# A two-model kernel on one core: other orders for the mixer's tiles, convolution taps, selection rounds and roots

## The reference

```python
def token_mixers(u, ...):                      # first block
    qa, ka, va, qi, ki, wi, qb, kb, vb, gate_a, gate_b = split(u @ w_in)
    # A: per query the 128 keys with the largest index scores (qi, ki, wi), then softmax attention, 8 heads
    # B: (softmax(q1 k1) - lam * softmax(q2 k2)) @ vb, 4 heads
    o_b = rms_norm(o_b, g_subln) * (1 - lam_init)        # over 128 features of a head
    return (sigmoid(gate_a) * (o_a @ w_branch_a) + sigmoid(gate_b) * (o_b @ w_branch_b)) @ w_out

def mixer(x):                                  # second block
    ua, ub, uc, ud = split(rms_norm(x) @ w_in)
    y_a = silu(layer_norm(depthwise_conv31(a * sigmoid(gate))))        # 31 taps, 256 channels
    y_b = rms_norm(bidirectional gated scan of (q, forget zf/zb, v), onorm) * silu(g)
    y_c = gb * depthwise_conv3(gc * xin)                               # 3 taps
    y_d = latent attention(cq, ckv, kr), 4 heads, q and k normed and rotated
    x = x + rms_norm per branch(y_a, y_b, y_c, y_d) @ w_out
    # then cross attention to mem with normed q and k, then the FFN
```

## Time and profile before

| what | us |
|---|---|
| median of 3 runs | 3483.81 (3483.07 to 3484.43) |
| the profiled execution, its own time | 3483.18 |
| its span in the trace | 3481.4 |
| each first-block layer: project, B, latent attention, tail | 165.5, 99.7, 90.7, 539.8 |
| each second-block layer: mixer, attention, tail | 249.7, 49.1, 534.1 (second layer 526.6) |

### The profile page before, as it was taken

One profiled execution on the slowest core, in us unless ns is written; L12 is line 12 of the kernel. 1 busy time (PEld: TensorE's weight loads), 2 busy tenths in 40 slices (PEclk: granted clock), 3 DMA queues, 4 the chain that ended last, 5 costly groups with the idle time before them and its releaser, 6 DMA issues. The chain is left out here.

```text
span 3481.4 us, 39157 instructions
## 1 busy us (share of the span) xinstructions
PE 3182.5 (91%) x14620; PEld 2474.4 (71%) x14620; DVE 1670.7 (48%) x2524; ACT 1435.2 (41%) x2281; POOL 1576.3 (45%) x870
## 2 busy tenths in 40 slices
PE   7978899999998799999999967899999985979999
PEld 6655688878766567887878735578887852758877
DVE  2773347731357533775235883433313785443320
ACT  4736533333384554333343454432223355352221
POOL 4623545544563354554456332334445432234443
PEclk8989999999899999999999978999999997989999
DMA  3111233323211112332322101223333200213333
GB/s 112 61 55 43 69 95 97 97 91 103 76 61 61 37 55 91 103 97 94 103 86 89 52 12 37 66 81 97 96 103 98 67 25 27 65 49 97 97 97 103
DMA packets 73740, 265.09 MB, mean 76 GB/s; under 512 B 8656, under 2 KB 9168, under 8 KB 73168
## 3 DMA queue, kind: packets, MB, share of 16 engines
q1 hardware_dynamic: 73552, 262.59, 24.1%
HBM read 260.46 MB, written 2.10 MB: 75 GB/s over the span
## 5 line engine op out<-in xcount | busy, mean ns | idle before, releaser
L359 POOL TENSOR_TENSOR low<-raw,high 128x1024 fp32r<-128x1024 f32 x482 | 1170.7, 2430 | 1298.8 <-ACT high L350 1276.0
L374 PE MATMUL bank<-slot_r,low 128*128 128x512 f32 (+2 forms) x3636 | 1434.6, 395 | 0.0
L375 PE MATMUL bank<-slot_r,high 128*128 128x512 f32 (+2 forms) x3636 | 1432.1, 394 | 0.0
L373 PE MATMUL bank<-slot_r,high 128*128 128x512 f32 (+1 forms) x3316 | 1339.9, 404 | 100.0 <-POOL low L359 22.5
L350 ACT ACTIVATE high<-raw 128x1024 fp32r<-128x1024 f32 x482 | 507.3, 1054 | 848.2 <-PE bank L375 819.1
L373 PEld LDWEIGHTS bank<-slot_r,high 128*128 128x128 f32 x3316 | 636.5, 192 | 286.5 <-issue 69.4
L374 PEld LDWEIGHTS bank<-slot_r,low 128*128 128x128 f32 (+1 forms) x3636 | 696.4, 192 | 148.9 <-issue 9.2
L375 PEld LDWEIGHTS bank<-slot_r,high 128*128 128x128 f32 (+1 forms) x3636 | 695.4, 191 | 149.8
L1568 DVE SCALAR_TENSOR_TENSOR tmp<-padded,small,tmp 128x512 f32<-128x512 f32 x176 | 209.9, 1251 | 0.0
L834 POOL TENSOR_SCALAR tmp<-tmp,stat 128x512 f32<-128x512 f32 (+3 forms) x128 | 72.0, 562 | 195.4 <-DVE stat L809 167.1
L698 PE MATMUL bank<-slots 64*128 64x256 f32 (+4 forms) x384 | 96.1, 509 | 44.5 <-PEq L320 40.7
(11 more groups left out here) (310 smaller groups left out, 3661.6 us busy)
## 6 DMA issues: line engine op xcount, KB each, us to landing
raw<-w SPq DMA_DIRECT2D x482, 512.0 KB, 3.5
slots<-x_in SPq DMA_DIRECT2D x4, 512.0 KB, 6.6
slots<-mem_in SPq DMA_DIRECT2D x2, 1024.0 KB, 4.9
out<-slots SPq DMA_DIRECT2D x8, 256.0 KB, 4.8
const<-const_in SPq DMA_DIRECT2D x1, 1073.5 KB, 10.6
padded<-p_in SPq DMA_DIRECT2D x2, 512.0 KB, 5.5
tmp<-masks_in SPq DMA_DIRECT2D x1, 512.0 KB, 11.4
small<-small SPq DMA_DIRECT2D x2, 231.5 KB, 2.7
```

The costliest lines, as they stand in the source:

```text
L359: pool.tensor_tensor(self.low[:, t % PARTS, :], self.raw[:, t % RING, :], self.high[:, t % PARTS, :].bitcast(F32), ALU.subtract).then_inc( ...
L373: pe.matmul(acc, lhs[0], rhs[1], start=first, stop=False)
L374: pe.matmul(acc, lhs[1], rhs[0], start=False, stop=False)
L375: return pe.matmul(acc, lhs[0], rhs[0], start=False, stop=last)
```

## The change

- `first_project` projects one more tile: gate tile 0, after the last four tiles, and DVE scales it at the end. From tile 8 on three selection rounds follow each tile instead of two, and 39 instead of 38 are done in this stage. `attention_b` has gate tiles 1 to 9, and its selection rounds move from the steps 2 to 11 to the steps 3, 5, 7 and 13 to 16.
- `attention_a` has 6 gate tiles instead of 7. Branch B's sums of squares come at steps 2 and 4, DVE copies them out, and ACT makes one Ln and one Exp over the four heads (128 x 2048) at step 6; products, high parts and remainders move with them.
- The mixer projects a and its gate first, then zf, zb, q, v, gc. The halves come one per tile for j = 13 to 18 and two for j = 19 to 23, instead of one per tile from 9 on. The taps come 5 per tile for j = 6 to 12, 2 for 13 to 18, none for 19 and 20, and 6 for 21 to 23, instead of 3 for 13 to 18, 5 for 19 to 23, 4 before the latent norms, and 15 in and after the heads. Branch C moves ahead of the heads; branch A's mean and variance move into the last jobs.
- Branch B's norm in the mixer (two reciprocals, two products on DVE and two on POOL) moves to `second_attention`, steps 2 and 4 on DVE.
- In `second_tail` the roots of key and query become Ln and Exp on ACT instead of Sqrt on ACT and a reciprocal on DVE; the seven `hf.add` (L520) move from DVE to POOL.

```diff
-    t = [list(range(starts[n] + c * P, starts[n] + c * P + P)) for n in ("zf", "zb", "q", "v", "a", "gate", "gc", "xin", "gb", "cq")
+    t = [list(range(starts[n] + c * P, starts[n] + c * P + P)) for n in ("a", "gate", "zf", "zb", "q", "v", "gc", "xin", "gb", "cq")
          for c in range(2)]
...
-    GATE = (40, 41, 42, 43, 44, 45, 46, 47, 52, 24, 25, 26, 56, 53, 54, 55)
+    GATE = (40, 41, 42, 43, 44, 45, 46, 47, 52, 53, 24, 25, 26, 56, 54, 55)
...
-    EARLY, WITH_B, SELECTED = 21, 9, 38
+    EARLY, WITH_B, SELECTED = 22, 9, 39
...
+                pe.wait_ge(sem("sin_done"), NR)
+                dense(pe, weights, banks[2][:, :], u_all)
...
+                weights.split_high(act, base + EARLY + 2)
...
-                        selection.rounds(2 if j < 11 else 3, (j - FIRST_IDX - 1) // 2)
+                        selection.rounds(3, (j - FIRST_IDX - 1) // 2)
                 selection.rounds(SELECTED - selection.done)
+                dve.wait_ge(sem("tile_done"), base + EARLY)
+                dve.tensor_tensor(S[:, GATE[0], :], banks[2][:, :], rs[:, :], ALU.mult).then_inc(sem("gate_scaled"), 1)
...
                 if step % 2 and step // 2 < WITH_B:
-                    gate_scale(dve, base, step // 2, GATE[step // 2])
-                if step >= 2:
-                    selection[0].rounds(1)
-                if step == 4 * 2 * NT // 2:
-                    gate_scale(dve, base, WITH_B - 1, GATE[WITH_B - 1])
-                    selection[0].rounds(selection[0].total)
+                    gate_scale(dve, base, step // 2, GATE[step // 2 + 1])
+                if step in (3, 5, 7) or step >= 4 * NT - 3:
+                    selection[0].rounds(1 if step < 4 * NT else selection[0].total)
+                if step == 4 * NT:
+                    gate_scale(dve, base, WITH_B - 1, GATE[WITH_B])
...
-        n_gates = 2 * KC - WITH_B
+        n_gates = 2 * KC - WITH_B - 1
...
-            if place == "turns" and step in (2, 4, 6, 8):
-                h = step // 2 - 1
+            if step in (2, 4) and place in ("scores", "turns"):
+                h = step - 2 + (place == "turns")
                 pe.wait_ge(sem("ob_square"), h + 1)
                 if h >= 1:
-                    pe.wait_ge(sem("ob_log"), h)
+                    pe.wait_ge(sem("ob_copied"), h)
                 pe.matmul(banks[6][:, :], cst("ones"), low[h], start=True, stop=True).then_inc(sem("ob_sum"), 1)
             if place == "values":
-                pe.wait_ge(sem("ob_log"), 4)
+                pe.wait_ge(sem("ob_copied"), 4)
             if place == "scores" and first_gate <= step < first_gate + 4 * n_gates:
...
-                act.activation(high[h], banks[6][:, :], ACT.Ln, scale=1.0 / P, bias=eps).then_inc(sem("ob_log"), 1)
-                act.wait_ge(sem("ob_log"), h + 1)
-                act.activation(high[h], high[h], ACT.Exp, scale=-0.5).then_inc(sem("ob_rstd"), 1)
-            if step in (5, 7, 9, 11):
-                h = (step - 5) // 2
+            if step == 6:
+                roots = wide(OB_PARTS[0][0])
+                act.wait_ge(sem("ob_copied"), 4)
+                act.activation(roots, roots, ACT.Ln, scale=1.0 / P, bias=eps).then_inc(sem("ob_log"), 1)
+                act.wait_ge(sem("ob_log"), 1)
+                act.activation(roots, roots, ACT.Exp, scale=-0.5).then_inc(sem("ob_rstd"), 1)
+            if step in (8, 9, 10, 11):
+                h = step - 8
                 act.wait_ge(sem("ob_normed"), h + 1)
                 act.activation(R[OB_PARTS[h][0]][:, :], S[:, OB + h, :], ACT.Copy).then_inc(sem("ob_high"), 1)
             if step >= first_gate and (step - first_gate) % 4 == 0:
@@ -1286,20 +1290,24 @@
...
-            if step in (4, 6, 8, 10):
-                h = step // 2 - 2
-                dve.wait_ge(sem("ob_rstd"), h + 1)
+            if step in (2, 3, 4, 5):
+                h = step - 2
+                dve.wait_ge(sem("ob_sum"), h + 1)
+                dve.tensor_copy(high[h], banks[6][:, :]).then_inc(sem("ob_copied"), 1)
+            if step in (7, 8, 9, 10):
+                h = step - 7
+                dve.wait_ge(sem("ob_rstd"), 1)
                 x = S[:, OB + h, :]
                 dve.scalar_tensor_tensor(x, x, col[:, SUB_GAIN:SUB_GAIN + 1], high[h], ALU.mult, ALU.mult).then_inc(sem("ob_normed"), 1)
             n = (step - first_gate - 3) // 4
             if step >= first_gate + 3 and (step - first_gate - 3) % 4 == 0 and n < n_gates - 1:
-                gate_scale(dve, base, n, GATE[WITH_B + n])
+                gate_scale(dve, base, n, GATE[WITH_B + 1 + n])
...
-            if n in (6, 8, 10, 12):
-                h = n // 2 - 3
+            if n in (9, 10, 11, 12):
+                h = n - 9
                 pool.wait_ge(sem("ob_high"), h + 1)
                 pool.tensor_tensor(R[OB_PARTS[h][1]][:, :], S[:, OB + h, :], R[OB_PARTS[h][0]][:, :].bitcast(F32), ALU.subtract).then_inc(sem("ob_low"), 1)
...
+        places = (rows[0:2] + [S[:, GA + c, :] for c in range(2)] + [S[:, F + c, :] for c in range(2)] + [S[:, F + 2 + c, ::-1] for c in range(2)]
+                  + [S[:, Q + c, :] for c in range(2)] + [S[:, V + c, :] for c in range(2)] + rows[2:4]
                   + [S[:, XIN + c, :] for c in range(2)] + [S[:, GB + c, :] for c in range(2)] + [S[:, CQ + c, :] for c in range(2)]
                   + [S[:, CKV, :], S[64:96, KR, :]] + [S[:, G + c, :] for c in range(2)])
-        AT_Q, AT_V, AT_A, AT_GA, AT_GC, AT_XIN, AT_GB, AT_CQ, AT_KR = 4, 6, 8, 10, 12, 14, 16, 18, 21
+        AT_A, AT_GA, AT_Z, AT_Q, AT_V, AT_GC, AT_XIN, AT_GB, AT_CQ, AT_KR = 0, 2, 4, 8, 10, 12, 14, 16, 18, 21
...
+        HALVES_AFTER = {13: 1, 14: 1, 15: 1, 16: 1, 17: 1, 18: 1, 19: 2, 20: 2, 21: 2, 22: 2, 23: 2}
...
-            first = j - FIRST_HALF_AT
-            if first < 0:
-                return []
-            return HALVES[first:first + 1] if j < N - 1 else HALVES[first:]
+            first = sum(HALVES_AFTER.get(i, 0) for i in range(j))
+            return HALVES[first:first + HALVES_AFTER.get(j, 0)]
...
+                    if j == 5:
+                        mean()
+                    if j == 7:
+                        variance()
...
-                mean()
-                variance()
...
+                            act.activation(S[:, B_R + c, :], banks[6 + c][:, :], ACT.Sqrt, scale=1.0 / 64, bias=eps).then_inc(sem("b_root"), 1)
                     if j >= 5:
                         key_root(j - 1)
+                    if j == 6:
+                        for c in range(2):
+                            act.wait_ge(sem("centered"), c + 1)
+                            act.activation(PT[:, 0, 2 + c, :], S[:, TAP_A + c, :], ACT.Square).then_inc(sem("centered_square"), 1)
+                    if j == 7:
+                        act.wait_ge(sem("var_summed"), 1)
+                        act.activation(PT[:, 1, 2, :], banks[7][:, :], ACT.Sqrt, scale=1.0 / 256, bias=eps).then_inc(sem("deviation"), 1)
                 key_root(len(jobs) - 1)
                 act.wait_ge(sem("v_projected"), 1)
                 for n in range(2):
                     act.activation(S[:, MV + n, :], banks[4 + n][:, :], ACT.Copy).then_inc(sem("v_evac"), 1)
-                for c in range(2):
-                    act.wait_ge(sem("centered"), c + 1)
-                    act.activation(PT[:, 0, 2 + c, :], S[:, TAP_A + c, :], ACT.Square).then_inc(sem("centered_square"), 1)
-                act.wait_ge(sem("var_summed"), 1)
-                act.activation(PT[:, 1, 2, :], banks[7][:, :], ACT.Sqrt, scale=1.0 / 256, bias=eps).then_inc(sem("deviation"), 1)
...
+                    if j >= AT_GA + 4:
+                        taps(5 if j < 13 else 2 if j < 19 else 0 if j < 21 else 6)
...
-                taps(4)
...
+                for tap_j in range(3):
+                    for c in range(2):
+                        tap(tap_j, c, 2, 1, "c_w", "c_b", S[:, Y + 4 + c, :], "tap_c")
+                for c in range(2):
+                    dve.wait_ge(sem("tap_c"), 5 + c)
+                    y = S[:, Y + 4 + c, :]
+                    dve.tensor_tensor(y, S[:, GB + c, :], y, ALU.mult).then_inc(sem("branch_c"), 1)
...
-                    if j < 4:
-                        taps(min(3, len(taps_a) - taps_done[0]))
-                    if j in (5, 6):
-                        c = j - 5
-                        r = PT[:, 0, c, :]
-                        dve.wait_ge(sem("b_root"), c + 1)
-                        dve.reciprocal(r, r).then_inc(sem("b_rstd"), 1)
-                        dve.wait_ge(sem("b_rstd"), c + 1)
-                        y = S[:, Y + 2 + c, :]
-                        dve.scalar_tensor_tensor(y, y, s2("onorm", c), r, ALU.mult, ALU.mult).then_inc(sem("b_normed"), 1)
-                taps(len(taps_a) - taps_done[0])
-                for tap_j in range(3):
-                    for c in range(2):
-                        tap(tap_j, c, 2, 1, "c_w", "c_b", S[:, Y + 4 + c, :], "tap_c")
```

(54 more changed lines are left out.)

15 lines of the change are left out of this document (4 added, 11 removed).

## The result

| | before | changed |
|---|---|---|
| median of 16 runs, us | 3482.94 (3481.74 to 3485.10) | 3489.90 (3485.61 to 3493.10) |
| ratio | | 1.0019, 95% interval 1.0012 to 1.0026 |
| span of the profiled execution, us | 3481.4 | 3485.8 |

The account below looks back on a forecast made before the run. PE was busy 91% of the span, leaving at most 299 us to order changes, with another limit in each stage. The terms sum to -4.9 a pass, -9.8 for two, taking 3483.8 to 3474 us; range 3448 to 3495.

Parts of the forecast that it names:

- Latent attention, -5.2: Latent attention, a pass: one wide Ln/Exp pair frees ACT and one gate tile leaves PE, -5.2 us, ends -8.5 and -2.
- The forecast's lower bound: Latent attention: the small end of the gain, -2 us, if products still wait for the wide root at step 6.
- The premise that only PE's idle time can be won or lost: Whole kernel: at most 299 us, some 9%, lie outside PE's work, and order changes can only act there.
- First block's tail, 0: First block's tail: no term in the forecast, so 0 us.
- Second attention: Second attention, a pass: the moved norm's reciprocals on DVE delay ACT's exponentials, +8 us, ends +6 and +9.5.
- mixer: Mixer, a pass: tiles +14 us from taps beside POOL splits and double halves; heads -17.2 from work leaving DVE.
- B's attention: B's attention, a pass: one selection round fewer, others moved, -1 us, ends -5 and +3.
- First projection: First projection, a pass: added gate tile fills PE's hole, DVE's tail shortens, -1.5 us, ends 0 and -3.
- Second tail: Second tail, a pass: fewer reciprocals, more table loads, adds moved to POOL, -2 us, ends -5 and +1.
- Free taps: Mixer's tiles take the taps for nothing, tile region +2 instead of +14, 3450 us; chance 0.22.
- Double halves that chill PE: Mixer tiles 19 and 20: waits before second halves drop PE's clock, tile region +25, 3496 us; chance 0.18.
- the third: Latent attention's pace is set elsewhere and tail loads cancel its gain: sum about +1, 3484 to 3486 us; chance 0.12.

Follow-up runs that it names:

- old roots: Changed kernel with branch B's latent-attention norm done per head again at steps 3 to 9 (four pairs of roots), gate tiles still from step 10: 3483.6 us.
- early gates and the wide root: Changed kernel with its one wide Ln/Exp pair kept, but latent attention's six gate tiles starting at step 6 instead of 10: 3485.3 us.
- both repairs: Changed kernel with per-head roots back in latent attention and the mixer's branch B norm at the end of the second attention: 3467.0 us, ratio 0.9952.

## Why the prediction went wrong

- **Latent attention, -5.2 against +2.6: the step that failed.** It said that ACT was busy without a break (it was, for 28.8 of the 30.5 us from 295.5 to 326), so that what ACT gives back moves PE forward, and the merged root entered the sum as no cost at all. ACT's busy time there was cover, not bound: leaving all roots out was worth 3.3 for 15 us of ACT. What bound, by the rows of the changed kernel, was the chain of one row from exponential through POOL's scale to PE's turn and ACT's copy. A block of 3.9 on ACT between two exponentials costs it little (gaps of up to 1.3 on PE), one of 6.5 made 7.55 of idle. With its bunched remainders the wide root cost 5.9 a layer, where the forecast had it make room for -5.2. The forecast's lower bound ("the products still wait for the wide root") looked at the products of the norm and not at the exponentials queued behind the root on ACT. The gate tile that left was right in sign and short in size: 90.7 to 87.3 with the old roots, 3.4 of the 5.2 forecast. -3.4 + 5.9 is the +2.6 of the table within 0.1. For two layers the step misses 15.6, more than the whole error of the spans' difference (+4.4 against -9.8, 14.2).
- **The premise that only PE's idle time can be won or lost.** The forecast set 299 us aside as all that a change of order can touch. After the change that idle time is 299.2, the same, and 4.1 of the 4.4 us by which the span grew stand in PE's busy time. PE's time for the same products is not fixed: 79.39 and 73.71 for one stage's 360, at a clock of 0.87 and 0.96.
- **First block's tail, 0 against +1.9.** No edit is there. The idle before the first products is the same 2.27 in both kernels, but the first stretch of the tail ran at a clock of 1.00 before and 0.69 after:

```profile
385.00:390.50 5.50, 5.01 (x22) 4.20 (x23) 4.11 (x3) 5.16 (x8) 4.47 (x3) 1.00 0.32 95
```

```profile
383.50:389.00 5.50, 4.94 (x15) 3.94 (x16) 4.09 (x3) 5.09 (x8) 4.40 (x3) 0.69 0.33 95
```

  The low clock over the tail lasted 20.5 us for 17.1, which is the difference. The kernel with early gates and the wide root had 20.5 in one layer and 17.1 in the other, with 541.4 and 539.8. The forecast had no term for it, and it could not be known from the edits.
- **Second attention (+7.1 for +8) and mixer (+13.8 and -16.8 for +14 and -17.2)** were right in mechanism and near in size. In the tiles the lag of the taps is 7.1 for 7.5, the halves 5.1 for 6 and the far scores -2.0 for -2.5; the 3.0 for colder PE and POOL's query level stand against 3.4 of longer PE busy time. In the heads the four k jobs and the end gave -13.8 for -13.1, the q half -2.2 for -4.1, and branch C in front of them cost nothing. In the second attention the forecast priced the delay of the exponentials alone; a part of the 7.1 was low clock.
- **The lock between DVE and POOL.** The Trainium skill (SBUF — State Buffer, "SBUF: two separate sides") has a DVE operation with two SBUF inputs and a GpSimd operation that reads SBUF exclude one another. The trace agrees: the taps under POOL's operations of 2.82 and 5.05 took 2.87 and 5.08, for 0.74 alone.
- **B's attention, -2.8 for -1:** the low clock there went from 12.8 to 6.8 us, about the difference. With the same code it lasted 13.7 in the kernel with both repairs, and the stage took 100.0 and 100.3, as before the change: the moved rounds by themselves gained nothing that shows. **First projection, -1.6 for -1.5:** the hole was filled as forecast (3.16 idle for 10.14), but the match of the lengths is luck, as other kernels with this code took up to 168.1, with 5.58 idle there. **Second tail, -2.1 for -2,** a mean of -4.1 and 0.0; PE's idle fell by 1.6 and 1.5. Its roots cost +1.0 (forecast +1.3), its adds gave -1.8 to -2.3 (forecast -3.3).
- **The rivals.** Free taps: no, by the 13.8. Double halves that chill PE: no, the late tiles kept PEclk 1.00 behind waits of 0.4 to 1.5. (The row that the forecast gave for such waits has 10.14 of idle; the near one is 2.94 in the earlier trace rows, behind which a product took 0.77.) The result is nearest to the third, that latent attention's pace is set elsewhere, which had 0.12 and was priced as no gain; that the root would cost was in no case. That the time fell inside the range is luck: its upper part was there for the second rival, which did not happen.

## To carry to other kernels

An engine that is busy through a stretch need not bound it: ask what waits behind the block that is to be merged, for how long the others can go on, and price the longest block and not the sum. Here, merging small operations to save table loads was worth little, since they lay between links of a chain, and it cost more than all of them together did. A norm whose result is needed late belongs behind the last link of the stage, where its engine idles to the barrier, not in the steps where it has free time on average.

## What the runs showed of the hardware

- Five 128x512 scalar_tensor_tensor with two SBUF inputs took 3.39 alone, 5.88 beside a copy and a split on POOL, and 12.30 beside a copy, a 2048-wide product and splits. One DVE operation is stretched per POOL operation, to its length. POOL's own operations were longer too in the same stretch (L359 2.82 to 2.84 for 2.40, L2222 5.05 for 4.61).
- The clock falls on identical work in one kernel or layer and not in another: 88.7 and 93.7 for the same stage. The changed kernel's 16 runs spread over 7.5 us and those of before over 3.4; ten runs of the one with old roots spread over 17.7 (3471.9 to 3489.6). An edit worth a few us in a stage needs the stage's own length and clock beside the total.
- Table loads before Ln and before Exp stayed apart in every form tried: 1.28 each, with one wide pair and with two.
